# Two chunks of the last output projection as one pair of columns, seven products of sums of blocks for eight in half of the feature blocks

## The reference

```python
def odd_layer(x, positions, norm_g, w_in, q_norm_g, w_q_up, kv_norm_g, w_kv_up, w_out):
    ...
    o = mla_attention(q_nope, q_rope, k_nope, k_rope, v)
    y = (o * jax.nn.silu(gate)) @ w_out
    return x + y
...
    return rmsnorm(x, final_norm)
```

## Time and profile before

| what | value |
|---|---|
| median of 3 runs | 815.97 us (815.49 to 816.03) |
| the profiled execution | 816.18 us, span 814.1 us |
| busy in the span | PE 804.1, DVE 462.9, ACT 411.3, POOL 111.7 us |
| HBM | 136.40 MB read, 170 GB/s over the span |

### The profile page before, as it was taken

The page is one execution under the profiler, slowest core; times in us unless marked ns, Lnnn a source line. Parts: engine busy times, 40 slices in busy tenths (PEclk is TensorE's granted clock), DMA queues, the critical chain, the costliest instruction groups (busy, mean ns, idle before and its releaser), DMA issues.

```text
span 814.1 us, 11934 instructions
## 1 busy us (share of the span) xinstructions
PE 804.1 (99%) x4204; PEld 688.6 (85%) x4204; DVE 462.9 (57%) x663; ACT 411.3 (51%) x613; POOL 111.7 (14%) x201
## 2 busy tenths in 40 slices
PE   9999999999999999999999999999999999999996
PEld 8878888888888888888888888888899999978885
DVE  5556666566445454646445655355557767754554
ACT  6644444445545464555445645445556555544442
POOL 6501121200001010031000010050000000000222
PEclk9999999999999999999999999999999999999998
DMA  9964564656666656553557666566554444435612
GB/s 313 294 186 143 161 176 134 177 155 169 194 182 170 178 167 181 173 187 105 186 198 211 176 186 186 156 193 189 157 155 143 130 158 164 157 109 176 197 61 103
DMA packets 77563, 139.10 MB, mean 171 GB/s; under 512 B 8968, under 2 KB 14256, under 8 KB 77392
## 3 DMA queue, kind: packets, MB, share of 16 engines
q1 hardware_dynamic: 76368, 137.21, 56.3%
q10 hardware_dynamic: 1152, 1.31, 0.5%
HBM read 136.40 MB, written 2.10 MB: 170 GB/s over the span
## 4 chain that ended last, share of the span: by engine, by line
PE 98%; issue 1%; DVE 0%; ACT 0%; POOLq 0%; POOL 0%; ACTq 0%; DVEq 0%
PE ps L1267 24%; PE ps L1269 24%; PE ps L1268 24%; PE ps L1638 2%; PE ps L1639 2%; PE ps L1637 2%; PE ps L1289 2%; PE ps L1445 2%; PE ps L1720 1%; PE ps L1680 1%; PE ps L1679 1%; PE ps L1681 1%; PE ps L1324 1%; PE ps L1402 1%; PE ps L1691 1%
## 5 line engine op out<-in xcount | busy, mean ns | idle before, releaser
L888 DVE TENSOR_TENSOR w_lo<-raw,w_hi 128x1024 fp32r<-128x1024 f32 x239 | 300.7, 1260 | 295.4 <-ACT w_hi L574 295.2
L574 ACT ACTIVATE w_hi<-raw 128x1024 fp32r<-128x1024 f32 x236 | 249.9, 1059 | 299.3 <-PE ps L1269 285.1
L1267 PE MATMUL ps<-w_hi,a_hi 128*128 128x512 f32 x868 | 341.6, 394 | 0.2 <-issue 0.2
L1269 PE MATMUL ps<-w_hi,a_lo 128*128 128x512 f32 x868 | 338.2, 390 | 0.0
L1268 PE MATMUL ps<-w_lo,a_hi 128*128 128x512 f32 x868 | 338.0, 389 | 0.0
L1269 PEld LDWEIGHTS ps<-w_hi,a_lo 128*128 128x128 f32 x868 | 162.9, 188 | 34.6
L1267 PEld LDWEIGHTS ps<-w_hi,a_hi 128*128 128x128 f32 x868 | 163.1, 188 | 33.6 <-DVE w_lo L888 0.8
L1268 PEld LDWEIGHTS ps<-w_lo,a_hi 128*128 128x128 f32 x868 | 163.1, 188 | 32.3
L1637 PE MATMUL ps<-a_hi,w_hi 128*128 128x256 f32 x160 | 45.8, 286 | 0.0
L1639 PE MATMUL ps<-a_lo,w_hi 128*128 128x256 f32 x160 | 45.3, 283 | 0.0
L1638 PE MATMUL ps<-a_hi,w_lo 128*128 128x256 f32 x160 | 45.3, 283 | 0.0
(11 more groups left out here) (255 smaller groups left out, 802.2 us busy)
## 6 DMA issues: line engine op xcount, KB each, us to landing
raw<-in_w_in_even SPq DMA_DIRECT2D x111, 512.0 KB, 3.7
raw<-in_w_in_odd SPq DMA_DIRECT2D x48, 512.0 KB, 3.7
raw<-in_w_out_even SPq DMA_DIRECT2D x32, 512.0 KB, 3.9
raw<-in_w_out_odd SPq DMA_DIRECT2D x32, 512.0 KB, 3.7
raw<-in_w_kv_up SPq DMA_DIRECT2D x16, 512.0 KB, 3.7
raw<-in_w_q_up SPq DMA_DIRECT2D x16, 384.0 KB, 3.3
xs<-in_x SPq DMA_DIRECT2D x6, 256.0 KB, 8.1
even<-in_final_norm SPq DMA_DIRECT2D x1, 1024.0 KB, 6.0
```

The source lines that it names most:

```text
L574: return a.activation(w_hi[:, ring, 0:w], raw[:, s, 0:w], ACT.Copy)
L888: return v.tensor_tensor(w_lo[:, ring, 0:w], raw[:, s, 0:w], w_hi[:, ring, 0:w].bitcast(F32), ALU.subtract)
L1267: m.matmul(acc, a_hi[:, k, tok], hi, start=first, stop=False)
L1269: ins = m.matmul(acc, a_lo[:, k, tok], hi, start=False, stop=last)
```

## The change

Chunks 1 and 2 (columns 512 to 1535, the second and the third of four) are made together. The feature blocks 0 to 7 are taken in pairs (k, k+1), so that a pair of feature blocks, the two token blocks and the two chunks form a 2x2 by 2x2 product of blocks. It is done with seven products of blocks, some of them of sums of blocks, for eight. Feature blocks 8 to 15 are done in the plain way, in between: a group is one such pair (15 products with the two plain blocks behind it), and there are four groups, numbered 0 to 3.

A piece of the pair is one feature block by 1024 columns (`pair_features` gives the block of piece q); of the first piece of a group only the first 512 columns are split. POOL makes the sums of tokens (8 operations of 256 columns, in chunk 0, from tokens that DVE puts together again with `tokens_whole`) and the sums of weights (`weight_sums`: four operations of 512 columns per group, into one buffer); ACT and DVE make high and low parts of them (`tokens_high`, `tokens_low`, `sums_high`, `sums_low`). PE's products go to banks 4 to 7 too; at the end ACT copies bank 4, DVE mixes banks 5 to 7 into the rows of token block 1 and into what POOL adds to token block 0 (`first_rows_mixed`). POOL's order changes: the residuals and gains of chunks 1 and 2 come behind all sums and mixing. SP's loop over the four chunks is written out, and a load into the slot of a piece that is summed waits for POOL's sums of it (`sums_taken`). `last_chunk` is as it was; it waits for the evacuation of banks 2 and 3.

```diff
+def pair_features(q):
+
+    return 2 * (q // 4) + q % 4 + (0 if q % 4 < 2 else NP - 2)
...
+            def pair_blocks(w, col, b, g):
+
+                for q in range(2 * NP):
+                    sp.wait_ge(lo_ready, b * NP + q + 1)
+                    if q >= NP and q % 4 < 2:
+                        sums_taken(4 * g + q // 4 - 2)
+                    sp.dma_start(raw[:, q % NP, :], w[:, pair_features(q), col:col + 2 * CW]).then_inc(raw_landed[q % NP], 16)
...
+                    if sums is not None and j % 4 < 2:
+                        sums_taken(sums + j // 4)
...
-            with sp.Fori(0, 4) as i:
-                block_of(wo1_d, i * CW, i + (B_OUT1 - 1))
+            block_of(wo1_d, 0, B_OUT1 - 1)
+            pair_blocks(wo1_d, CW, B_OUT1, 0)
+            block_of(wo1_d, 3 * CW, B_OUT1 + 2, sums=2)
...
-            pool.wait_ge(fin_landed, 16)
-            for n in range(3):
-                add_residual(C_OUT1, n)
...
+            def weight_sums(parts, b, gm):
+
+                q = 4 * (gm % 4)
+                if gm == 0:
+                    pool.wait_ge(t_done, 2 * U_LAST + 2)
+                if gm % 4:
+                    pool.wait_ge(w_sum_low, 2 * gm)
+                for s in (q, q + 1):
+                    pool.wait_ge(raw_landed[s % NP], b * 16 + (16 if s < NP else 32))
+                (w11, w12), (w21, w22) = ((raw[:, s % NP, 0:CW], raw[:, s % NP, CW:]) for s in (q, q + 1))
+                s1, s3, s2, s4 = (parts["w_sum"][:, CW * n:CW * n + CW] for n in range(4))
+                for n, (dst, x0, x1) in enumerate(((s1, w11, w12), (s3, w12, w22), (s2, s1, w22), (s4, s2, w21))):
+                    if n >= 2:
+                        pool.wait_ge(w_summed, 4 * gm + (1 if n == 2 else 3))
+                    g.tensor_tensor(dst, x0, x1, ALU.add).then_inc(w_summed, 1)
...
+            def first_rows_mixed(parts, gr, n):
+
+                u, w = parts["mixed"][:, 0:CW], parts["mixed"][:, 2 * CW:3 * CW]
+                x1, x2 = xs[:, 0, CW * n:CW * n + CW], xs[:, 0, CW * n + CW:CW * n + 2 * CW]
+                pool.wait_ge(first_mixed, gr + 1)
+                step(g.tensor_tensor(x1, x1, u, ALU.add))
+                pool.wait_ge(mixed_ready, 4 * gr + 3)
+                step(g.tensor_tensor(x2, x2, w, ALU.subtract))
+
+            for s in range(2):
+                token_sums(out1_pair, s)
+            weight_sums(out1_pair, B_OUT1 + 1, 0)
+            pool.wait_ge(fin_landed, 16)
+            add_residual(C_OUT1, 0)
+            weight_sums(out1_pair, B_OUT1 + 1, 1)
+            final_gains(0)
+            for m in (2, 3):
+                weight_sums(out1_pair, B_OUT1 + 1, m)
+            first_rows_mixed(out1_pair, 0, 1)
+            for n in (1, 2):
+                add_residual(C_OUT1, n)
+            for n in (1, 2):
+                final_gains(n)
...
-            outputs(B_OUT1, C_OUT1, 4, (
-                {1: [lambda: z_prep(1)], 2: [lambda: weights_out(None)], 3: [lambda: z_prep(2)], 5: [lambda: z_prep(3)]},
-                {5: [stream_squares(0, C_OUT1, 4, 32)]},
-                {5: [stream_squares(1, C_OUT1, 4, 32)]},
-                {3: [stream_squares(2, C_OUT1, 4, 32)]}), part="out", end=True)
...
+            def sums_high(parts, gm):
+
+                if gm % 4:
+                    act.wait_ge(w_sum_used, gm)
+                for i in range(2):
+                    cols = slice(1024 * i, 1024 * i + 1024)
+                    act.wait_ge(w_summed, 4 * gm + 2 * i + 2)
+                    a.activation(parts["w_hi"][:, cols], parts["w_sum"][:, cols], ACT.Copy).then_inc(w_sum_high, 1)
+
+            def pair_piece(parts, b, gr, q):
+
+                piece(b, q, CW if q % 4 == 0 else FULL)
+                if q % 4 == 1:
+                    sums_high(parts, 4 * gr + q // 4)
...
+            b, c, parts, added = B_OUT1, C_OUT1, out1_pair, 4
+            first_plan = {1: [lambda: z_prep(1)], 2: [lambda: weights_out(None)], 3: [lambda: z_prep(2)], 4: [lambda: tokens_high(parts, 0)],
+                          5: [lambda: z_prep(3)], 6: [lambda: tokens_high(parts, 1)]}
+            ahead(b, pieces=4, between=first_plan)
+            for q in range(2 * NP):
+                for fn in first_plan.get(q + 4, []):
+                    fn()
+                if q == 3:
+                    act.wait_ge(res_added, 1 + added)
+                    evac(0, c, stg[0][:, 0, :], part="out")
+                if q == 4:
+                    stream_squares(0, c, added, 32)()
+                pair_piece(parts, b + 1, 0, q)
+            for k in range(2):
+                piece(b + 3, k)
+            act.wait_ge(piece_used, (b + 1) * NP + 14)
+            a.activation(parts["mixed"][:, 0:CW], ps[:, 4, :], ACT.Copy).then_inc(first_mixed, 1)
+            for n in range(2):
+                act.wait_ge(res_added, n + 2 + added)
+                pair_evac(b, 0, n, stg[1 - n][:, 0, :])
+            for k in range(2, 4):
+                piece(b + 3, k)
+            ahead(b + 3, pieces=4, between={1: [stream_squares(1, c, added, 32)], 3: [stream_squares(2, c, added, 32)]})
...
-            outputs(B_OUT1, C_OUT1, (
-                {1: [lambda: z_prep(1)], 2: [lambda: weights_out(PAIRS, last=True)], 3: [lambda: z_prep(2)], 4: [last_weighted], 5: [lambda: z_prep(3)]},
-                {}, {}, {}), part="out", end=True)
...
+            def tokens_whole(parts, us, gs):
+
+                s = gs % 2
+                dve.wait_ge(t_free_d, freed(us[s]) + 2)
+                if s:
+                    dve.wait_ge(tok_summed, gs)
+                v.tensor_tensor(parts["tok"].rearrange("p (k q) -> p k q", k=4), a_hi[:, 4 * s:4 * s + 4, :].bitcast(F32),
+                                a_lo[:, 4 * s:4 * s + 4, :].bitcast(F32), ALU.add).then_inc(tok_whole, 1)
...
+            def sums_low(parts, gm):
+
+                for i in range(2):
+                    cols = slice(1024 * i, 1024 * i + 1024)
+                    dve.wait_ge(w_sum_high, 2 * gm + i + 1)
+                    v.tensor_tensor(parts["w_lo"][:, cols], parts["w_sum"][:, cols], parts["w_hi"][:, cols].bitcast(F32),
+                                    ALU.subtract).then_inc(w_sum_low, 1)
+
+            def pair_piece(parts, b, gr, q):
+
+                piece(b, q, CW if q % 4 == 0 else FULL)
+                if q % 4 == 1:
+                    sums_low(parts, 4 * gr + q // 4)
...
+            b, c, parts = B_OUT1, C_OUT1, out1_pair
+            first_plan = {0: [lambda: tokens_whole(parts, STEPS_Z, 0)], 1: [lambda: z_prep(1)],
+                          2: [lambda: weights_out(PAIRS, last=True), lambda: tokens_whole(parts, STEPS_Z, 1)], 3: [lambda: z_prep(2)],
+                          4: [last_weighted, lambda: tokens_low(parts, 0)], 5: [lambda: z_prep(3)], 6: [lambda: tokens_low(parts, 1)]}
+            ahead(b, pieces=4, between=first_plan)
+            for q in range(2 * NP):
+                for fn in first_plan.get(q + 4, []):
+                    fn()
+                if q == 3:
+                    dve.wait_ge(piece_used, pieces_through(c, "out"))
+                    dst = xs[:, 1, 0:CW]
+                    v.tensor_tensor(dst, dst, ps[:, 1, :], ALU.add).then_inc(evac_d, 1)
+                pair_piece(parts, b + 1, 0, q)
+            u, u2, w, u3 = mixed(parts)
+            x1, x2 = xs[:, 1, CW:2 * CW], xs[:, 1, 2 * CW:3 * CW]
+            dve.wait_ge(first_mixed, 1)
+            v.tensor_tensor(u2, u, ps[:, 6, :], ALU.subtract).then_inc(mixed_ready, 1)
+            dve.wait_ge(mixed_ready, 1)
+            v.tensor_tensor(u3, u2, ps[:, 7, :], ALU.add).then_inc(mixed_ready, 1)
+            v.tensor_tensor(w, u2, ps[:, 5, :], ALU.add).then_inc(mixed_ready, 1)
+            dve.wait_ge(mixed_ready, 3)
+            v.tensor_tensor(x1, x1, u3, ALU.add).then_inc(second_mixed, 1)
+            piece(b + 3, 0)
+            dve.wait_ge(second_mixed, 1)
+            dve.wait_ge(pair_done, 1)
+            v.tensor_tensor(x1, x1, ps[:, 3, :], ALU.add).then_inc(evac_d, 1)
+            v.tensor_tensor(u2, u3, ps[:, 5, :], ALU.add).then_inc(mixed_ready, 1)
+            dve.wait_ge(mixed_ready, 4)
+            v.tensor_tensor(x2, x2, u2, ALU.subtract).then_inc(second_mixed, 1)
+            piece(b + 3, 1)
+            dve.wait_ge(second_mixed, 2)
+            dve.wait_ge(piece_used, (b + 3) * NP)
+            v.tensor_tensor(x2, x2, ps[:, 1, :], ALU.add).then_inc(evac_d, 1)
+            for k in range(2, 4):
+                piece(b + 3, k)
+            ahead(b + 3, pieces=4)
...
+                def triple(acc, hi, lo, w, x, first, last=False):
+                    m.matmul(acc, hi, w, start=first, stop=False)
+                    m.matmul(acc, hi, x, start=False, stop=False)
+                    return m.matmul(acc, lo, w, start=False, stop=last)
...
+                pe.wait_ge(evac_a, c - 1)
+                pe.wait_ge(evac_d, c - 1)
+                step_free(last_step + 1)
+                pe.wait_ge(tok_low, 2 * gr + 2)
```

(81 more changed lines are left out.)

23 lines of the change are left out of this document (22 added, 1 removed).

## The result

The changed kernel takes 819.32 us (median of 5, 818.93 to 820.23), the kernel before 815.97; the ratio is 1.0044, with a 95% interval of 1.0032 to 1.0056. So it is slower by 3.35 us, where 4.1 were forecast and 814.0 to 823.5 was the range.

What follows compares the result with a forecast made beforehand. PE was taken to bound the kernel (busy 99%), with DVE and POOL taking turns. Terms -2.72 + 1.0 + 3.1 + 2.8 = +4.1 gave a median of 820.1 us, range 814.0 to 823.5.

Steps and rivals of the forecast that it cites:

- The matmuls: In the pair's four groups, seven products for eight remove 12 matmuls from PE's path: -2.72 us.
- Opening: Chunk 0 and the pair's start: a stall grows by about 0.3 and token sums' low half comes 0.7 late: +1.0 us.
- The groups: Pair's groups: 11.5 us of DVE and POOL turns in 10.2 us make PE wait for weight sums: +3.1 us.
- turns between low parts and sums: DVE operations with two SBUF inputs and POOL's two-input ones alternate by whole instruction; handover costs POOL 1.16 us, DVE 1.08.
- End of the pair: Before last_chunk PE waits 1.9 us for DVE's evacuation, then 0.9 for the second piece's low part: +2.8 us.
- Loads and POOL's tail: SP's second-half loads waiting for weight sums, and POOL's gains and squares before DVE's mean, stay hidden: no cost.
- A: Groups: if a sum costs 1.04 us, a turn fits and the groups' term is 0: 816.1 us; chance 0.18.
- B: DVE and POOL: the taking of turns is an accident or they overlap, so faster: 814.4 us; chance 0.10.
- C: PE's clock falls after waits of 1 to 2 us, adding 4 us: 824; chance 0.08.

Runs made afterwards that it cites:

- e_gdve: Changed kernel: last-chunk low parts and evacuation before mixing; weight sums (groups 1 to 3) and gains (chunks 1, 2) on DVE; token sums' parts earlier; 814.06 us.
- e_tiny: The changed kernel with POOL's weight sums of 8 columns in place of 512, all waits, conversions and products kept: 817.09 us.
- e_memset: The changed kernel with each POOL weight sum of groups 1 to 3 replaced by memsets about as long that read nothing from SBUF: 817.58 us.
- e_bcast: The changed kernel with the second input of each weight sum being one column read over and over: 818.17 us.
- e_dve: The changed kernel with the weight sums of groups 1 to 3 made by DVE, not POOL: 817.34 us.
- e_end: The changed kernel with the last chunk's first two low parts and bank 3's evacuation put ahead of DVE's mixing of banks 5 to 7: 818.00 us.
- e_eight: The changed kernel with one product of each group done twice, putting 12 matmuls back: 820.34 us.

## Why the prediction was right, step by step

- **The matmuls, -2.72.** 12 fewer, clock as before, pitch within 0.002 us. Right, but only e_gdve gets most of it.
- **Opening, +1.0; measured +1.47** (chunk 0 from its first matmul to the pair's first: 27.83 us before, 29.30 after). The first wait of the pair, 0.7, is there (0.73), and the stall at L1489 grew from 0.73 to 0.91, where 0.3 more was said; with sums of 8 columns it is 0.73 again (e_tiny). The term is 0.5 short by a wait that I had left out of the layout: the transposes at L1891 wait for DVE's low part of `z_prep(1)` (0.61 us), which stands behind low part 4. That one takes 1.77 us and ends 1.07 us after POOL's third token sum, as in a turn; no run takes the token sums away, so this is read from rows alone:

```profile
716.77 1.77 DVE L1020 TENSOR_TENSOR w_lo<-raw,w_hi 128x1024 fp32r<-128x1024 f32 x1 [1.64 <-ACT w_hi L658]
718.47 1.28 DVE L1051 TENSOR_TENSOR a_lo<-ps,a_hi 128x512 fp32r<-128x512 f32 x2
...
716.73 0.74 POOL L592 TENSOR_TENSOR ys<-ys,work 128x256 f32<-128x256 f32 x1
```

- **The groups, +3.1; measured 2.4** (from the pair's first matmul to the last chunk's, 43.52 us before and 45.25 after, with the 2.72 of matmuls added and the 2.00 of the last wait taken off). Of it 1.42 and 0.45 are the two waits; the rest is matmuls that start anew behind a wait, and tenths spread over the pair. The mechanism, turns between low parts and sums, is shown by e_memset, e_bcast, e_tiny and e_dve, each of which takes the waits away by another side of it. The size was too large where I let every sum meet an operation of DVE: sums 1 ran from 743.93 to 751.40, 7.5 us and not 8.4, as DVE was waiting for ACT twice in that time, so group 1 was not late at all. The gains behind them took 4.5 us (L616) where 3.6 was said, since both gave a turn away; the two errors cancel, and that group 2's wait was near, 1.42 for 1.6, is in part luck. Sums 2 took 8.4 (755.83 to 764.27), as said; group 3's wait was 0.45 for 0.75. DVE's waits for ACT in sums 1:

```profile
746.03 0.72 DVE L1020 TENSOR_TENSOR w_lo<-raw,w_hi 128x512 fp32r<-128x512 f32 x1 [0.98 <-ACT w_hi L658]
748.09 2.16 DVE L1020 TENSOR_TENSOR w_lo<-raw,w_hi 128x1024 fp32r<-128x1024 f32 x1 [1.33 <-ACT w_hi L658]
```

- **End of the pair, +2.8; measured 2.9.** 1.9 and 0.9 were said; 2.00 and 0.58 came, and a few tenths of new starts. e_end shows both to be DVE's order.
- **Loads and POOL's tail at no cost.** PE and ACT wait for no DMA in the stage, and the last of POOL's chain (L645) ends at 803.14, where DVE's L1433 is at 806.01. Right.
- **Sum.** -2.72 + 1.47 + 2.4 + 2.9 = +4.05, as the stage has it, and 3.35 in the medians; +4.1 was forecast. Two of the terms were off by 0.5 and 0.7 with opposite signs, so the total is nearer than its parts, and that much of it is luck. Of the 0.7 us between stage and medians 0.60 lies ahead of the stage in the two profiled executions, where nothing was changed; why it does, no run shows.
- **Rivals.** A is not what happened, but its condition is real: at 1.04 us a sum the groups don't wait (e_bcast). Its 816.1 us is not, since opening and end cost what they cost: e_bcast takes 818.17. The Trainium skill's rate (GPSIMD Engine Reference, section 3.1), by which a sum was an estimated 1.1 us, pointed to that side; the chip takes 1.27, and L623 after (1.29). B is refuted by the low parts of 1.9 us and more beside POOL's sums, and by what e_memset and e_dve gain. C's clock did not fall in the profile after (1.00 from 785 to 795 us), but it did in one execution of e_memset, behind the same wait, at a price of 1.6 us and not 4.
- **What I had not weighed:** that DVE could do the sums itself. I had costed work by engine, and the free engine was the dear one.

## What to carry to other kernels

Before moving elementwise work to an idle POOL, add it to DVE's own load if both read two tensors from SBUF, and compare the sum with the time that the stage gives: here 11.5 us in 10.2 made PE wait, and the same sums on DVE (8.8 in 10.2) did not. Near the limit the sum of the prices doesn't decide: e_bcast has 10.6 us (DVE's 6.4 and four sums of 1.04) in 10.2, and PE did not wait. There the turn laid out step by step (9.8 us in rival A) was the better guide. Count what a saved matmul is worth by what PE waits for next: with twelve put back, the stage grew by little more than a quarter of their time. At a change of banks, put what the next chunk waits for (its first pieces, the evacuation) ahead of mixing that nobody waits for.

## What the runs showed of the hardware

- A two-input operation of POOL on 512 columns takes 1.27 us with two full inputs and 1.04 when one of them is a single column read over and over (the first two weight sums, which meet no turn: 2.53 us after, 2.04 in e_bcast).
- The same wait of 1.84 us of idle PE (about 2.0 us late) left the granted clock at 1.00 in the changed kernel, e_eight, e_bcast, e_tiny and e_dve, and was followed by 0.50 for three microseconds in e_memset, 1.6 us of cost. Each of these is one profiled execution; no run shows what set e_memset's apart, or whether the wait was the cause. e_gdve, which has no such wait, shows 1.00 from 741 to 799 us.
